# Product 5 of the projection groups in quarters, with its weight sums, its scratch loads and the rotation's steps laid round it

## Reference, cut to what matters

```python
h = rmsnorm(x, norm_g)                       # x: 1024 tokens x 1024
proj = h @ w_in                              # 1024 x 1024 by 1024 x 12288
b_a, c_a, x_a, z_a, q, k, v, z_b, g_a, g_b = split(proj)
y_a = (b_a * (conv3(c_a * x_a) + conv_b) * silu(z_a)) @ w_a_out
o   = retention(rotary(q), rotary(k), v)     # 4 heads, chunks of 128
y_b = (rmsnorm(o) * silu(z_b)) @ w_b_out
out = rmsnorm(x + (sigmoid(g_a) * y_a + sigmoid(g_b) * y_b) @ w_o) * final_g
```

## Time and profile before

| what | value |
|---|---|
| median of 3 runs | 1365.33 us (1364.96 to 1366.29) |
| profiled execution | 1364.82 us, span 1363.0 us |
| TensorE busy | 1351.7 us, 99% |
| VectorE busy | 1037.9 us, 76% |
| ScalarE, GpSimd busy | 607.5 us, 350.8 us |
| granted TensorE clock | 0.998 |
| conv group, turn group | 37.18 us, 37.58 us from start to start |

### The profile page before, as it was taken

One profiled execution on the slowest core, in us unless ns is written; L12 is line 12 of the kernel. 1 busy time (PEld: TensorE's weight loads), 2 busy tenths in 40 slices (PEclk: granted clock), 3 DMA queues, 4 the chain that ended last, 5 costly groups with the idle time before them and its releaser, 6 DMA issues.

```text
span 1363.0 us, 17225 instructions
## 1 busy us (share of the span) xinstructions
PE 1351.7 (99%) x6642; PEld 1143.1 (84%) x6642; DVE 1037.9 (76%) x1089; ACT 607.5 (45%) x823; POOL 350.8 (26%) x341
## 2 busy tenths in 40 slices
PE   9999999999999999999999999999999999999997
PEld 8788888888888888888888888888888888888886
DVE  7898466677777777677877777748776998788887
ACT  7843233433333333333433333438778443434445
POOL 0100122343444444223222233325544001100002
PEclk9999999999999999999999999999999999999999
DMA  9736545334443343466656556767767699935443
GB/s 343 214 126 213 152 107 169 89 103 109 109 109 84 102 108 94 131 177 177 178 157 174 149 156 183 216 209 252 269 217 263 151 331 306 237 152 201 165 83 124
DMA packets 112978, 234.80 MB, mean 172 GB/s; under 512 B 7680, under 2 KB 50816, under 8 KB 108032
## 3 DMA queue, kind: packets, MB, share of 16 engines
q1 hardware_dynamic: 104112, 194.87, 42.0%
q0 software_dynamic: 8640, 38.80, 16.0%
q10 hardware_dynamic: 144, 0.02, 0.0%
HBM read 169.70 MB, written 55.57 MB: 165 GB/s over the span
## 4 chain that ended last, share of the span: by engine, by line
PE 92%; ACT 2%; DVE 2%; issue 2%; DMA 1%; POOL 1%; SPq 1%; POOLq 0%; ACTq 0%; DVEq 0%
PE psum L2591 15%; PE psum L2593 15%; PE psum L2594 15%; PE psum L2732 7%; PE psum L2734 7%; PE psum L2733 7%; PE psum L2517 3%; PE psum L2519 3%; PE psum L2518 3%; PE psum L2506 3%; PE psum L2509 3%; PE psum L2508 3%; PE psum L2636 2%; PE psum L2638 2%; PE psum L2637 2%
## 5 line engine op out<-in xcount | busy, mean ns | idle before, releaser
L1126 ACT ACTIVATE slots<-work 128x1024 fp32r<-128x1024 f32 (+1 forms) x166 | 169.5, 1027 | 418.5 <-PE psum L2594 284.8
L2591 PE MATMUL psum<-hc,slots 128*128 128x512 f32 x912 | 354.9, 389 | 0.0
L2593 PE MATMUL psum<-hc,slots 128*128 128x512 f32 x912 | 354.9, 389 | 0.0
L2594 PE MATMUL psum<-hc,slots 128*128 128x512 f32 x912 | 354.8, 389 | 0.0
L2594 PEld LDWEIGHTS psum<-hc,slots 128*128 128x128 f32 x912 | 171.2, 188 | 35.7
L2591 PEld LDWEIGHTS psum<-hc,slots 128*128 128x128 f32 x912 | 171.3, 188 | 34.9
L2593 PEld LDWEIGHTS psum<-hc,slots 128*128 128x128 f32 x912 | 171.2, 188 | 34.8
L1412 ACT ACTIVATE last_slot<-arena 128x1024 fp32r<-128x1024 f32 x112 | 118.6, 1062 | 163.1 <-PE psum L2734 157.3
L2732 PE MATMUL psum<-last_slot 128*128 128x512 f32 (+1 forms) x452 | 175.3, 388 | 0.0
L2734 PE MATMUL psum<-last_slot 128*128 128x512 f32 (+1 forms) x452 | 175.0, 387 | 0.0
L2733 PE MATMUL psum<-last_slot 128*128 128x512 f32 (+1 forms) x452 | 175.0, 387 | 0.0
(11 more groups left out here) (225 smaller groups left out, 2424.1 us busy)
## 6 DMA issues: line engine op xcount, KB each, us to landing
work<-w_channel SPq DMA_DIRECT2D x80, 512.0 KB, 4.3
work<-w_channel POOLq DMA_DIRECT2D x40, 512.0 KB, 5.5
arena<-w_last SPq DMA_DIRECT2D x19, 1024.0 KB, 7.4
qk<-qk_scratch SPq DMA_DIRECT2D x32, 512.0 KB, 3.5
arena<-w_last POOLq DMA_DIRECT2D x9, 1024.0 KB, 11.0
v_raw<-value_scratch SPq DMA_DIRECT2D x32, 256.0 KB, 3.8
arena<-gate_scratch SPq DMA_DIRECT2D x16, 512.0 KB, 6.6
value_c<-w_value SPq DMA_DIRECT2D x10, 512.0 KB, 4.7
```

The lines of the kernel that those rows point to most:

```text
L1126: nc.scalar.activation(slots[:, u % SLOTS, 0, 0:columns_of(u)], src, ACT.Copy, scale=-1.0 if negated(u) else 1.0).then_inc(w_hi, 1)
L2591: nc.tensor.matmul(bank, slot[:, 0, w], x_high, start=product in STARTS and j == 0, stop=False, skip_group_check=True)
L2593: nc.tensor.matmul(bank, slot[:, 0, w], x_low, start=False, stop=False, skip_group_check=True)
L2594: last = nc.tensor.matmul(bank, slot[:, 1, w], x_high, start=False, stop=j == 3, skip_group_check=True)
```

## The change

Product 5 is done in quarters in groups 2 to 18 (`FIFTHS`). What comes with it:

- a new unit (`FIFTH_HALF`) behind product 5's first, and its splits, sums and waits, laid anew in every engine's order;
- `hx` now serves products 5 and 4 in turn. Both sets of T1, T2, T4 are kept in DRAM (`hx_d`), and SyncE loads one of them (T4 512 KB, T1 and T2 1024 KB) twice a group: for product 5 once product 4 of the group before is done, for product 4 once product 5 is done. TensorE waits for these loads;
- in groups 0 and 1 the second sums of product 5's activations are made and stored (four quarter sums, four T sums, four low parts on VectorE, four copies on ScalarE);
- S1 is no longer a GpSimd sum from group 1 on: SyncE loads quadrant 3 into e and GpSimd's queue adds quadrant 2 by an accumulating DMA;
- GpSimd makes product 5's four small sums ahead of the conv gate's second product, and product 4's before product 3's;
- the rotation: steps 1 to 4 of the first half move ahead by one product, of the second half steps 0, 1 go behind product 6's sum, 2 behind product 5's, and 3, 4, 5 behind product 7's sum; `turned` moves back by one product for both halves.

```diff
+FIFTHS = range(2, GROUPS - 1)
+UNIT_TABLE = [(g, p) for g in range(GROUPS) for p in (0, 1, 2, 3, FIFTH_HALF, 4, 5, 6, LAST_HALF, THIRD_HALF)
...
+    return product == 4 and g in TWICE or product == 3 and g in THIRDS or product == 5 and g in FIFTHS
...
@@ SyncE
+            if g in FIFTHS:
+                sp.wait_ge(unit_done, ended_at(g - 1) + 1)
+                load_hx(5)
...
-                sp.wait_ge(w_ready, unit_at(g, 5) + 1)
-                load_work(g + 1, "d", 3)
+                sp.wait_ge(w_ready, fifth_ended_at(g) + 1)
+                load_work(g + 1, "e", 3)
                 sp.wait_ge(w_ready, unit_at(g, 7) + 1)
                 load_work(g + 1, "b", 2)
                 if g in THIRDS and g > THIRDS.start:
                     stores[kind_of(g - 1)](g - 1)
+                if g in FIFTHS:
+                    sp.wait_ge(unit_done, fifth_ended_at(g) + 1)
+                    load_hx(4)
...
@@ GpSimd
+            if g:
+                work_loaded(g, "e")
+                pool.dma_start(work[ROLES[g]["e"]][:, :], w_channel[g, 2], accum_op=ALU.add).then_inc(s1_in, 16)
...
+            if g in FIFTHS:
+                second_sums(g, 5)
+            if conv:
                 conv_gate(g - 1, 2)
+            if g in FIFTHS:
+                s1(g + 1)
...
@@ VectorE, at unit u; (g, n) is unit u - 1
                 if n in (5, 6) and halved_product(g, product_at(n)):
                     second_first(g, product_at(n))
+                    if n == 6 and g in FIFTHS and g not in THIRDS:
+                        low(u + 1)
+                elif n == 3 and halved_product(g, 5):
+                    second_first(g, 5)
+                elif n == FIFTH_HALF:
+                    second_rest(g, 5, range(1))
+                    if g in THIRDS:
+                        low(u + 2)
+                    second_rest(g, 5, range(1, 3))
+                    add(g, 5)
+                    if g not in THIRDS:
+                        low(u + 2)
...
+                if u >= VALUE_UNITS and place_of(u)[1] == 5 and place_of(u)[0] in FIFTHS and place_of(u)[0] - 1 in QZS:
+                    for step in (3, 4, 5):
+                        turn(place_of(u)[0] - 1, 1, step)
                 low(u + 2)
...
-                    for step in {0: (0,), 2: (1, 2, 3, 4, 5)}.get(p, ()):
+                    for step in ({0: (0,), 1: (1, 2, 3, 4), 2: (5,)} if g in FIFTHS else {0: (0,), 2: (1, 2, 3, 4, 5)}).get(p, ()):
                         turn(last, 0, step)
-                    if p == 3:
+                    if p == (4 if g in FIFTHS else 3):
                         turned(last, 0)
-                    for step in {3: (0, 1, 2, 3), 4: (4, 5)}.get(p, ()):
+                    for step in ({2: (0, 1), 4: (2,)} if g in FIFTHS else {3: (0, 1, 2, 3), 4: (4, 5)}).get(p, ()):
                         turn(last, 1, step)
-                    if p == 4:
+                    if p == (5 if g in FIFTHS else 4):
                         turned(last, 1)
...
@@ TensorE
+            if product != 3 and g in FIFTHS:
+                pe.wait_ge(t4_in, 16 + 16 * hx_loads(g, product))
             product_of_quarters(u, 2, second(product, "T4"), direct_quarter(g, product, 2)).then_inc(unit_done, 1)
...
+            if product != 3 and g in FIFTHS:
+                pe.wait_ge(t1_t2_in, 16 + 16 * hx_loads(g, product))
             product_of_quarters(u, 2, second(product, "T1"), psum[:, z + 1, 0:QUARTER], start=True)
```

More of the change, by code:

```diff
@@ L342, in build @@
     t4_sums = sb("t4_sums", CONS_AT + 8 * KB, [P, 4, 2, QUARTER])
+    t5_high, t5_low = (sb(f"t5_{n}", TP_AT[1] + m * 8 * KB, [P, 4, 2, QUARTER]) for m, n in enumerate(("high", "low")))
     t3_quarters = sb("t3_quarters", CONS_AT, [P, 4, 2, QUARTER])
@@ L715, in _ @@
                 stores[kind_of(g - 1)](g - 1)
+            if g + 1 < GROUPS and g not in THIRDS:
+                sp.wait_ge(w_ready, ended_at(g) + 1)
+                load_work(g + 1, "d", 3)
             if g == QZS.start:
@@ L1533, in _ @@
                 third_high("T3")
-            if g == THIRDS.start and p == 4:
+            if g == THIRDS.start and p == FIFTH_HALF:
                 third_high("T1")
@@ L1560, in _ @@
                 first_tap(g - 1)
-            if p == 3:
+            if p == (FIFTH_HALF if g in FIFTHS and kind == "conv" else 3):
                 c11(g)
+            if g == CONVS.start and p == 1:
+                act.wait_ge(conv_step, 1)
+                nc.scalar.activation(u_pad[:, 0:CONV - 1], u_pad[:, 0:CONV - 1], ACT.Silu)
             if kind == "gate":
@@ L2076, in _ @@
             if u >= VALUE_UNITS and place_of(u)[1] == 2 and place_of(u)[0] - 1 in CONVS:
-                for n in range(1, CONV):
+                if place_of(u)[0] in FIFTHS:
+                    dve.wait_ge(summed, second_summed(place_of(u)[0], 5, 4))
+                conv_tap(place_of(u)[0] - 1, 1)
+                if place_of(u)[0] in FIFTHS:
+                    low(u + 2)
+                for n in range(2, CONV):
                     conv_tap(place_of(u)[0] - 1, n)
@@ L2083, in _ @@
                     low(u + 2)
+            elif u >= VALUE_UNITS and place_of(u)[0] in FIFTHS and place_of(u)[1] in (0, 1, 2, 3, 4, 6, FIFTH_HALF):
+                conv = place_of(u)[0] - 1 in CONVS
+                if place_of(u)[1] == 0 or place_of(u)[1] in (1, 2) and not conv:
+                    low(u + 2)
+                if place_of(u)[1] == 0 and conv:
+                    low(u + 3)
+                if place_of(u)[1] == FIFTH_HALF:
+                    low(u + 1)
+                    low(u + 2)
             elif u + 2 < UNITS and (u < VALUE_UNITS or place_of(u)[1] != LAST_HALF):
+                if u >= VALUE_UNITS and place_of(u)[1] == 5 and place_of(u)[0] in FIFTHS and place_of(u)[0] - 1 in QZS:
+                    for step in (3, 4, 5):
+                        turn(place_of(u)[0] - 1, 1, step)
                 low(u + 2)
@@ L2560, in unit @@
                 pe.wait_ge(kept_in, 80)
+            if product == 5 and g == FIFTHS.stop:
+                pe.wait_ge(fifth_kept, 192)
             if product == 3 and g == THIRDS.stop:
@@ L2705, in _ @@
                     first_half(g, product)
+                    if product == 5:
+                        second_half(g, 5)
                     if product == 4:
```

189 lines of the change are left out of this document (130 added, 59 removed).

## The result

The change made the kernel slower: 1372.49 us (median of 6 runs, 1371.28 to 1374.84) against 1365.21 (6 runs, 1364.96 to 1366.29), ratio 1.0054 with the interval 1.0043 to 1.0065. Predicted were 1359.8 us and a range up to 1364.5. The mark that the prediction set for itself, TensorE waiting for a DMA, is what the profile shows.

A forecast was written before the change was run, and what follows sets the result against it. TensorE's number and width of matmuls was taken to bound groups 0 to 19. 1364.8 (profiled) - 8.7 saved + 3.2 turn-group waits = 1359.3, with 0.5 for the median 1359.8 us; the range takes in 1356.3 and reaches 1364.5.

The forecast's parts named there:

- The mark that the prediction set for itself: Sign that the prediction is wrong: TensorE waits for a DMA; others were certain new gaps or turn groups above 38 us.
- I cost it at nothing: Conv groups: product 4's hx set lands at 29 to 30 us, T1 is wanted at 31.0, so no cost.
- hx late in the conv groups: Rival: product 4's hx set lands 0.5 us past the need in eight conv groups, giving 1363.8 us; chance 0.10.
- the price of its cover: Conv groups: without cover for the hx set, each microsecond past 31.0 us costs 8 us.
- The end of a turn group: Groups 11 to 18: VectorE's list ends at 37.4 us, TensorE wants it at 37.0; 0.4 us wait each, 3.2 us.
- the port's: Turn group's end: VectorE's `turned` and step 2 meet GpSimd's small sums at the shared port, adding 1.0 us.
- the 0.42 and 0.54 us of the earlier trace: Group 14: extra time of 0.69 us VectorE operations beside small sums, read as little over half a sum per meeting.
- SyncE's stores behind `turned`: Turn groups: SyncE's later wait holds four stores, d and product 5's set; landing 5 to 8 us into next group, harmless.
- 0.51 us per product: Groups 2 to 18: product 5 in quarters takes 4.93 us instead of 5.44, saving 8.7 us over 17 groups.
- VectorE's load: Per group, VectorE gains 3.4 us of work: 30.9 of 36.7 us in conv groups, 32.8 of 37.1 in turn groups.
- no wait at all: Rival: in turn groups `turned` and small sums miss each other or the list is 0.4 us shorter; 1356.6 us, chance 0.26.
- The rival that ended on the slower side: Hx transfers late everywhere: TensorE waits 1.4 us in 17 groups, 24 us against 8.7, giving 1380.6 us; chance 0.08.

The follow-up runs named there:

- run 2: Changed kernel with the store of y issued behind product 4's two hx loads in conv groups: 1366.72 us, ratio 1.0011 to the kernel before.
- run 3: Changed kernel with S1's accumulating DMA issued behind product 4's small sums in conv groups: 1365.6 us, ratio 1.0005 to the kernel before.
- Run 1: Changed kernel without the hx loads and TensorE's waits for them (output leaves out separate second sums): 1363.85 us, ratio 0.9991 to the kernel before.
- run 7: Changed kernel with both the store of y behind product 4's hx set and S1's accumulating DMA behind product 4's small sums in conv groups: 1364.44 us.
- Run 4: Changed kernel with the second `turned` moved behind the split of the next group's product 1 in groups 11 to 18: 1381.77 us, ratio 1.0122.
- Run 6: Changed kernel with a one-element sigmoid added in group 18, so ScalarE's table load falls earlier, in idle time: 1373.55 us, ratio 1.0056.
- run 9: Changed kernel with conv groups' y store and S1 DMA later, product 4's first-half split early in turn groups, product 5 whole in group 18: 1356.93 us.
- Run 5: Changed kernel with the split of product 4's first half moved ahead of two of product 5's pieces in turn groups and group 18: 1370.01 us.
- run 11: Changed kernel without hx loads and with product 4's first-half split early in turn groups and 18 (output leaves out separate second sums): 1357.52 us.
- run 12: The kernel of run 9 with product 5 in quarters in group 18 too: 1360.19 us, ratio 0.9963 to the kernel before the change.
- run 8: Changed kernel with y store and S1 DMA later, product 4's split early, table load early, product 5's old quarter copied back early: 1362.47 us.

## Why the prediction was wrong

**The step that failed: "I cost it at nothing", of the hx loads.** The need was right (31.0 us into a conv group). The landing was put at 29 to 30; in groups 3 to 9 it was 31.4 to 32.9. Two terms were off. The set was expected to go out at 21.4; T4 did, but T1 and T2 behind it only at 22.0. The transfers from b on, 6.6 to 7.5 us at 350 to 400 GB/s with 2 us on it, were put at 8.6 to 9.5 us from 20.3. They took 11.1 to 12.6: in group 5 12.05 us at 283 GB/s. The rate came from a stretch of plain loads, while here b's load, y's store and S1's accumulating DMA lay beside. How much each of these lowers the rate, no run tells; moved away, they take 0.9 and 1.8 us off the landing (runs 2 and 3). Run 1 prices the whole at 8.6 us, and run 7 shows that order alone gives back 8.1 of it. The rival "hx late in the conv groups" had the right mechanism and 0.10 of the chance; by its 0.5 us a group it had half of the true price. The prediction had also set the price of its cover, 8 us for each microsecond past 31.0: in the seven groups the set landed 0.4 to 1.9 us past it, 0.9 on the mean, and they paid 7.5.

**The end of a turn group: mechanism right, size off.** Predicted was one gap of 0.4 us ahead of product 1; there are 0.17 us of wait, 0.15 us ahead of T2 and a slower start, 0.7 us together in seven groups, 4.8 us, where 3.2 were predicted for eight. The term that was too small is the port's: 1.0 us for three meetings, measured 1.3. With it the list ends at 37.74 us where 37.4 was predicted; without it at 36.4, as predicted. Its reading was also wrong. The prediction took the 0.42 and 0.54 us of the earlier trace rows as half a block. The rows fit a whole block of which the first part had passed: at 754.15 the first small sum, held until then by L2032, has 0.6 us to go, L2034 waits for that and then runs its 0.6, and the second small sum waits in turn, so that it shows 1.18 for 0.73. In the kernel before it was the same. L1915 started ahead of the first small sum (709.59, 1.11 us), and L1918 (710.14) waited for what was left of it:

```profile
709.42 0.69 DVE L1915 TENSOR_TENSOR turn_b<-tp_v,rope_sb 128x512 f32<-128x512 f32 x1
```

Run 4 has the long case, 2.20 us added beside S2. The rule that the prediction named from the Trainium skill, "SBUF — State Buffer", section "Who interferes with whom", that the later operation blocks until the first is through, agrees with all of these rows.

**Group 18 was missing.** It was counted as one more group with a wait of 0.4 us, and lost 2.0. Its copy of product 2's banks is a sigmoid, which brings a table load of 1.28 us on ScalarE ahead of product 3's split. The old list had 2.2 us of room at its end. Run 6 moves the load to an idle stretch and the group is 1.42 us shorter.

**Group 19 was missing too.** The prediction followed SyncE's stores behind `turned` only to the next group's loads, and not to the first qk load, which waits for all of them. It went out 12.9 us into group 19 before and 19.5 after. That used up its room, and costs a wait of 0.9 us in the changed kernel and up to 4.0 in its variants, where from 2.2 us on the clock falls too.

**What was right.** 0.51 us per product; the groups' own lengths give 8.2 us for the 8.7 predicted. VectorE's load was near: 30.6 us in a conv group where 30.9 was predicted, 33.8 in a turn group where 32.8 was. The meetings account for that: the 29.36 us of before hold 1.4 of them, the 33.8 hold 2.7, as the small sums of product 5 meet rotation steps in the middle of the group too, where VectorE has slack. One slip in its working costs nothing: the second half of a product in quarters has 1024 weight columns (24 matmuls against 18) and not 768, so the splits add 0.95 us and not 0.68; the list of the end has the right 1.14 for it. The run without waits, 9, is at 1356.9 with group 18's product 5 whole; the rival "no wait at all" had 1356.6. Thus 14.3 us of waits in groups 3 to 18, not the arithmetic, made the change slow. The rival that ended on the slower side named the same transfers, with waits in all groups; they came in the conv groups, where the room was smallest and not where the DMA engines were fullest.

**What stays open.** Run 5's late store in group 14 was seen in one profile; that such stalls make up the scatter of its runs is likely but not shown. Whether it is the 3 MB or their place in SyncE's queue that makes qk late is open too. The profiles of runs 9 and 11 have no such stall, but run 9 still loads the sets in the turn groups with the DMA engines at 0.94, so the room there is thin.

## To carry to other kernels

A load that is issued when its buffer comes free and wanted 9 us later has no cover until its landing time is read beside the traffic that will be there: move stores and accumulating DMAs out from beside it first. When a product gets shorter by half a microsecond in each of 17 groups, follow every edge group to its end (a table load, the first load of the next stage), since a wait there can cost more than several products save: group 18 in quarters saves 0.5 us and costs 3.3 (run 12 against run 9). Put a GpSimd sum beside VectorE operations with an input in PSUM, by moving the split that releases it.

## What was not expected of the hardware

- A VectorE operation with both inputs in SBUF that starts behind a GpSimd sum lasts until that sum is through and then its own time: 1.23 us for 0.68 beside sums of 0.73, and 2.88 beside one of 2.4. Beside VectorE sums with an input in PSUM the same GpSimd sums took 0.73 and cost nothing.
- With 313.5 MB instead of 234.8 moved in the execution, loads of 512 KB land after 5.7 instead of 4.3 us, and accumulating ones after 7.2 instead of 5.5. Moving one neighbour away took 0.9 us (the store of y) or 1.8 us (S1's accumulating DMA) off a landing of 9.6 (1024 KB, medians of conv groups 3 to 9).
- After TensorE had stood for 4.0 us (run 4) the granted clock was 0.84, then 0.50 over 5 us, and back at 0.98; after 3.0 us (run 5) it was 0.85 and 0.81, after 2.8 us (run 8) 0.68 in one stretch, after 2.2 us (run 6) 0.82 and 0.84. After 1.8 us (run 5, at qk) and 1.5 us (run 12) it stayed at 1.00.
